# Routing of the last two fetched tiles moved from the decide stage into the dense stage

## What is computed

```
q  = (t @ wq) as 8 heads x 2 halves
sc = q . subkeys                      # 8 x 2 x 128 scores
sv, si = top_k(sc, 16)                # best 16 of each half
cand = sv[half 0][:, None] + sv[half 1][None, :]
cv, ci = top_k(cand, 16)
e  = si0[ci // 16] * 128 + si1[ci % 16]   # 8 x 16 expert numbers below 16384
g  = softmax(cv)
h  = u[e] . t ;  a = gelu(h) * g ;  out = sum a * v[e]
```

## Time and profile before

| | us |
|---|---|
| median of 3 runs | 4033.78 (4032.9 to 4043.76) |
| profiled execution | 4026.89 |
| its span | 4025.2 |

### The profile page before, as it was taken

One profiled execution on the slowest core, in us unless ns is written; L12 is line 12 of the kernel. 1 busy time (PEld: TensorE's weight loads), 2 busy tenths in 40 slices (PEclk: granted clock), 3 DMA queues, 4 the chain that ended last, 5 costly groups with the idle time before them and its releaser, 6 DMA issues. The chain is left out here.

```text
span 4025.2 us, 44686 instructions
## 1 busy us (share of the span) xinstructions
PE 3549.7 (88%) x14147; PEld 2107.2 (52%) x14147; DVE 2617.7 (65%) x5036; ACT 841.0 (21%) x1599; POOL 1631.8 (41%) x1245
## 2 busy tenths in 40 slices
PE   8997878776699999988862899999999999999998
PEld 6445567776457667656651344444444444444443
DVE  0451878883405435344464988888888878888886
ACT  1451211112423444354510000010001000010001
POOL 0000077770000777777773433334333334333331
PEclk9899889887799999999986999999999999999999
DMA  7793399995765656666856999999999999999994
GB/s 256 315 408 146 105 383 407 384 391 210 254 222 185 151 128 160 143 138 116 169 123 250 391 406 388 388 400 405 400 416 403 397 372 400 388 398 388 382 387 186
DMA packets 424246, 1201.21 MB, mean 298 GB/s; under 512 B 150473, under 2 KB 215417, under 8 KB 345337
## 3 DMA queue, kind: packets, MB, share of 16 engines
q0 software_dynamic: 168496, 680.80, 45.8%
q1 hardware_dynamic: 187600, 505.84, 34.2%
q10 hardware_dynamic: 67968, 12.45, 1.9%
HBM read 1127.33 MB, written 72.68 MB: 298 GB/s over the span
## 5 line engine op out<-in xcount | busy, mean ns | idle before, releaser
L2066 POOL DMA_INDIRECT d_ring<-peer_uv,d_idx x512 | 655.4, 1280 | 1087.6 <-DVEq L2120 981.9
L2223 PE MATMUL d_ps<-d_xd,d_u 128*128 128x512 f32 x2048 | 908.5, 597 | 99.9 <-DMA d_u<-u_blocks 81.1
L2234 PE MATMUL d_ps<-d_v,d_a 128*128 128x512 f32 x2048 | 914.1, 600 | 43.3 <-DVE d_a L2126 36.5
L1512 POOL DMA_INDIRECT G<-c_cellg,c_cell x384 | 617.5, 1608 | 436.6 <-DVE c_cellg L1641 233.5
L2118 DVE SCALAR_TENSOR_TENSOR d_acc<-d_ring,d_aw,d_acc 128x1024 f32<-128x1024 f32 x512 | 657.7, 1285 | 102.1 <-DVE d_acc L2118 66.9
L2223 PEld LDWEIGHTS d_ps<-d_xd,d_u 128*128 128x128 f32 x2048 | 391.8, 192 | 596.0 <-issue 584.3
L2234 PEld LDWEIGHTS d_ps<-d_v,d_a 128*128 128x128 f32 x2048 | 393.3, 193 | 545.5 <-issue 544.8
L2106 DVE SCALAR_TENSOR_TENSOR d_ring<-d_ring,d_xn 128x1024 f32<-128x1024 f32 x512 | 605.9, 1221 | 97.3 <-DMA d_qacc<-ys 51.5
L840 POOL DMA_INDIRECT a_x<-peer_uv,a_rowu x128 | 154.2, 1205 | 547.8 <-DVE a_rowv L910 505.3
L2188 ACT ACTIVATE d_ge<-d_h (+1 forms) x256 | 52.0, 203 | 1204.9 <-DVE d_ring L2106 1204.6
L1037 PE MATMUL a_ps<-a_w_low,a_x_high 128*128 128x256 f32 (+1 forms) x704 | 204.3, 290 | 61.7 <-DVE a_w_low L852 45.8
(11 more groups left out here) (360 smaller groups left out, 4134.4 us busy)
## 6 DMA issues: line engine op xcount, KB each, us to landing
c_chunk<-wq SPq DMA_DIRECT2D x128, 512.0 KB, 5.0
d_u<-u_blocks SPq DMA_DIRECT2D x128, 512.0 KB, 18.7
d_v<-v_blocks SPq DMA_DIRECT2D x128, 512.0 KB, 16.5
s_kc<-sb_kT SPq DMA_DIRECT2D x32, 1024.0 KB, 9.5
s_vc<-sb_v SPq DMA_DIRECT2D x32, 1024.0 KB, 7.4
c_chunk<-w_m SPq DMA_DIRECT2D x64, 512.0 KB, 5.5
d_gb<-G SPq DMA_DIRECT2D x32, 1024.0 KB, 34.5
G<-b_zeros SPq DMA_DIRECT2D x32, 768.0 KB, 8.3
```

The source lines that it names most:

```text
L1512: pool.indirect_dma_start(out=grid, out_offset=bass.IndirectOffsetOnAxis(ap=cell[q][:, s:s + 1], axis=0), in_=cell_g[q][:, s:s + 1], in_of ...
L2066: pool.indirect_dma_start(out=ring[:, b], out_offset=None, in_=a["peer_uv"], in_offset=bass.IndirectOffsetOnAxis(ap=idx8[par][:, b:b + 1], ...
L2223: last = nc.tensor.matmul(ps[:, HB + x % 2, :], ub[j][:, k], xd[:, k].rearrange("p t q -> p (t q)"), start=(k == 0), stop=(k == KC - 1))
L2234: last = nc.tensor.matmul(ps[:, VB + c % 4, :], A[u][j][:, q * P:(q + 1) * P], vb[u][j][:, half * 512:half * 512 + 512], start=(j == 0), s ...
```

## The change

VectorE no longer routes turns 7 and 8 in decide. ScalarE moves their scores into two tiles of their own (`late`), without waiting for VectorE, and stores them to memory, 1 MB each. In dense, ScalarE loads the first at the start and the second in block 14 into a tile that shares memory with the second token and sum buffers. VectorE runs the same routing steps in 15 pieces for each tile (`choose`), one at the end of each of blocks 0 to 14 (first of the two tiles) and 16 to 30 (second), writing into `idx` and `gw` directly. For that the first fetched tile is no longer a loop: its 32 blocks are written out on VectorE and ScalarE. The second tile's token and sum loads (`xn[1]`, `acc[1]`) wait until both tiles are routed (`chosen`). The results of gelu and weight are kept in place (`h`, `gw`) in place of tiles of their own. The third and fourth fetched tiles (GIVEN = 2 onwards) are the two concerned. SP's load of `gw` is cut to the first two tiles like that of `idx`, and the small table `digit` is loaded as well.

The 15 pieces of one tile are: 0 and 3, 16 max each; 1 and 4, 16 max_index; 2, 16 match_replace; 5, the three candidate sums; 6, 8 max and 8 max_index; 7, 8 match_replace and 8 max; 8, 8 max_index and the shift for the softmax; 9, ten small steps; 10 and 12, a one-hot test and its multiply over 2048 elements; 11 and 13, the reduction (13 also forms the expert number); 14, the sum, reciprocal and weights.

```diff
@@ decide @@
+        late = [sb(f"c_late{n}", [P, 16, P]) for n in range(2)]
 (SP)
-                routed(NT - 2)
-                routed(NT - 1)
 (VectorE)
                 normed(NT - 1)
-                halves_best(NT - 2)
-                pairs_best(NT - 2)
-                experts_of(NT - 2)
-                weigh(NT - 2)
-                halves_best(NT - 1)
-                pairs_best(NT - 1)
-                experts_of(NT - 1)
-                weigh(NT - 1)
 (ScalarE)
                 def scores_of(j):
-                    if j > 1:
+                    to = late[j - NT + 2] if j >= NT - 2 else sc
+                    if 1 < j < NT - 2:
                         act.wait_ge(dve_r.sem, dve_r.at(j - 1, "sum2"))
...
+                    if j >= NT - 2:
+                        act.wait_ge(act_r.sem, act_r.at(j, "sc3"))
+                        act.dma_start(o["late"][j - NT + 2], to[:]).then_inc(late_st, 16)
...
-                softmax(NT - 2)
                 scores_of(NT - 1)
-                softmax(NT - 1)
+                act.wait_ge(late_st, 32)
@@ dense @@
+        xa = sb("d_xa", [P, 4, D])
+        xn, acc = [xa[:, 0], xa[:, 2]], [xa[:, 1], xa[:, 3]]
+        late = xa[:, 2:4].rearrange("p u (r n) -> p (u r) n", n=P)
                 if T == 0:
-                    body(T, 0)
-                with eng.Fori(1 if T == 0 else 0, TB // BODY) as i:
-                    body(T, first + i)
+                    for k in range(TB // BODY):
+                        body(T, k)
+                else:
+                    with eng.Fori(0, TB // BODY) as i:
+                        body(T, first + i)
 (SP)
-                sp.dma_start(idx[:], o["idx"].rearrange("t p s -> p t s")).then_inc(rows_in, 16)
+                sp.dma_start(idx[:, 0:GIVEN], o["idx"][0:GIVEN].rearrange("t p s -> p t s")).then_inc(rows_in, 16)
 (GpSimd)
                 for T in range(FETCHED):
+                    if T >= GIVEN:
+                        pool.wait_ge(chosen, 2 * (T - GIVEN) + 1)
...
+                    if T == 0:
+                        pool.wait_ge(chosen, 4)
+                        pool.dma_start(xn[1], o["xn"][1]).then_inc(xn_in, 16)
+                        pool.dma_start(acc[1], o["ys"][DENSE + 1]).then_inc(acc_in, 16)
 (VectorE)
+                def choose(j, n):
...
+                    if n < 5:
+                        if n == 0:
+                            dve.wait_ge(eps_done, 3)
+                            dve.wait_ge(late_in, 16 * (j + 1))
+                        best(16, sc, top, top_i, ("top1", "cut", "top2", "topi"), j, n)
...
                             if m:
                                 add_rows(T, hb - 1, slots(m - 1), col - 2)
+                        if number(k):
+                            n = BODY * k + x
+                            choose(n // 16, n % 16)
 (ScalarE)
+                act.dma_start(late, o["late"][0]).then_inc(late_in, 16)
...
                         small_gelu(hb + 1, col + 2)
+                        if number(k) and BODY * k + x == 14:
+                            act.wait_ge(dve_r.sem, dve_r.at(0, "sum2"))
+                            act.dma_start(late, o["late"][1]).then_inc(late_in, 16)
+                        if number(k) and (BODY * k + x) % 16 == 9:
+                            j = (BODY * k + x) // 16
+                            act.wait_ge(dve_r.sem, dve_r.at(j, "shift"))
+                            nc.scalar.activation(gw[:, GIVEN + j], gw[:, GIVEN + j], ACT.Exp).then_inc(act_g, 1)
```

More of the change, by code:

```diff
@@ L1995, in dense @@
         prod_done, row_gelu, weighed, summed = sem("d_prod_done"), sem("d_row_gelu"), sem("d_weighed"), sem("d_summed")
+        chosen, late_in = sem("d_chosen"), sem("d_late_in")
+        dve_r = Steps(sem("d_dve_route"), "top1 cut top2 topi cand0 cand1 cand2 ctop1 ccut ctop2 ctopi shift "
+                      "topf mid high col low mid2 high2 rest place rise hot1 pick1 sum1 hot2 pick2 sum2 cell expert", 0)
+        act_g, dve_g = sem("d_act_softmax"), Steps(sem("d_dve_softmax"), "gsum grecip", 0)
         rms, recip, scaled = sem("d_rms"), sem("d_recip"), sem("d_scaled")
@@ L2042, in _ @@
                     v_rows(j, 0, j)
-                for dst, src in ((gw[:], o["gw"].rearrange("t p s -> p t s")), (gf[:], bass.AP(a["gf"].tensor, 0, [[0, P], [1, D]]))):
+                for dst, src in ((gw[:, 0:GIVEN], o["gw"][0:GIVEN].rearrange("t p s -> p t s")), (digit[:], a["digit"]), (gf[:], bass.AP(a["gf"].tensor, 0, [[0, P], [1, D]]))):
                     sp.dma_start(dst, src).then_inc(tabs, 16)
@@ L2099, in _, with step, best @@
                 dve.sem_inc(v_taken, LEAD)
-                dve.wait_ge(tabs, 32)
+                nc.vector.memset(top_f[:], 0.0).then_inc(eps_done, 1)
+                dve.wait_ge(tabs, 48)
+                def step(ins, j, name=None):
+                    ins.then_inc(dve_r.sem, 1)
+                    if name:
+                        dve.wait_ge(dve_r.sem, dve_r.at(j, name))
+                def best(n, src, vals, idx, names, j, stage):
+                    if stage == 0:
+                        for h in range(n):
+                            last = nc.vector.max(vals[:, h, 0:8], src[:, h])
+                        step(last, j, names[0])
+                    elif stage == 1:
+                        for h in range(n):
+                            nc.vector.max_index(idx[:, h, 0:8], vals[:, h, 0:8], src[:, h])
+                    elif stage == 2:
+                        for h in range(n):
+                            last = nc.vector.match_replace(src[:, h], vals[:, h, 0:8], src[:, h], LOW)
+                        step(last, j, names[1])
+                    elif stage == 3:
+                        for h in range(n):
+                            last = nc.vector.max(vals[:, h, 8:16], src[:, h])
+                        step(last, j, names[2])
+                    else:
+                        for h in range(n):
+                            last = nc.vector.max_index(idx[:, h, 8:16], vals[:, h, 8:16], src[:, h])
+                        step(last, j, names[3])
@@ L2140, in body @@
                         b = BODY * k + x
-                        if not (number(k) and x == 0):
+                        if not (number(k) and k == 0 and x == 0):
                             y = (x - 1) % BODY
```

97 lines of the change are left out of this document (78 added, 19 removed).

## The result

The changed kernel takes 4087.41 us in the median (4079.69 to 4090.63) against 4038.77 for the kernel before (4032.9 to 4044.38, measured beside it). The ratio is 1.0121, with a 95% interval of 1.0102 to 1.0141: **49 us slower**, between 41 and 57. Forecast were 4081 us and 47.5 us on top.

A forecast was written before the change was run, and what follows sets the result against it. TensorE was taken to set the dense stage's pace, with VectorE close behind and DMA nearly full. Starting VectorE 12.7 us earlier and adding 60.2 in the first tile gave +47.5 us, 4081 us in the median, range 4053 to 4115.

The forecast's parts named there:

- The first tile is VectorE's: First fetched tile: VectorE becomes the bound, 401.3 us of its own plus 93.0 + 3 for pieces; tile grows 60.2 us.
- The exit: End of decide: with the routing gone the scatters are late next; it comes about 14.7 us earlier, between 8 and 15.
- one of its own signs: End of decide, in the changed kernel's profile: wrong if the exit is later than 2142 or earlier than 2125.
- the 6.9 us of excess: End of decide: time of scatters and gaps over 1.54 and 0.3 us during VectorE's routing, forecast to go away.
- The opening: Start of dense: 2.6 us more for the score load, 0.6 less for index and weight tables, net +2.0 us.
- No cost in the other steps: First tile's Exp calls, second score load, delayed second-tile loads: 0 us; tiles two to four: no change, give or take 10.
- The relief: First fetched tile: straight code cuts VectorE's own time from 437.1 to 401.3 us, 35.8 us less.
- The scatters' excess staying (1): End of decide: long scatters stay long, so the exit gives 8 us in place of 14.7; 4088 us, chance 0.10.
- The pieces sinking into idle time (2): First fetched tile: VectorE's 62.2 us of idle time takes pieces, tile grows only 31 us; 4052 us, chance 0.06.
- The other side (3): First fetched tile: TensorE stays the bound because pieces cost under 48.5 us in place of 93; 4011 to 4021, chance 0.04.
- The clock (4): First fetched tile: TensorE's waits let its clock fall, 55 us on top; 4136 us, chance 0.05.
- Instruction supply (5): First fetched tile: long unrolled code pays a 6.6 us turn's worth some six times, 40 us; 4121 us, chance 0.05.

## Why the prediction was right, point by point

**The first tile is VectorE's: right.** 60.2 us of growth were forecast and 492.0 - 437.1 = 54.9 measured, and 492.0 to 492.3 in every profile that has the 30 pieces. The structure of the sum (401.3 us of its own, plus the pieces, against TensorE's bound) was tested from three sides: no pieces gives 427, half of them 446, all of them 492. The mis-sized term is the pieces: 93.0 + 3 us forecast, 492.0 - 401.3 = 90.7 measured, 45.4 a tile. Half of them gives nearly the same: 445.8 - 401.3 = 44.5. Most of the miss is the 3 us for the pieces' last waits, for which no time shows; the rest is the 46.5 us elapsed in the earlier trace rows, of which VectorE was busy for 45.6.

**The exit: right in kind, too large in size.** That the scatters are late next is shown by the pair with fewer of them. Forecast were 14.7 us (8 and 6.9 add up to 14.9). Measured are exits of 93.9, 86.2, 99.5, 87.0 and 88.4 us in the five profiles without routing there, against 102.4 to 103.4 in five with it: 3 to 17 us less, 12 in the mean (91.0 against 103.0). By one of its own signs the prediction failed: the first load was to go out between 2125 and 2142, and it went out at 2148.0 and 2151.3. The residual sum before it was 10 and 21 us later than in the trace that the forecast started from; but the sign made no room for that, nor did the forecast say how far the scatters follow it.

Three things were mis-sized.
- Behind the last scatter's start lie 6.4 us before the first load (2141.65 to 2148.03), where I had allowed 3. I had taken the gap of 2.01 us before the scatter at 2088.74 for a landing. But the program waits for landings only before the first of each 16 scatters, and this one is the ninth of its 16, the 361st in all. The gap stands there in all 12 profiles, with or without routing, and takes 1.9 to 5.9 us.
- For the same reason the 1.7 us of that gap, counted in the 6.9 us of excess, did not go away. The other 5.1, the long scatters themselves, did: after 2050 the first profile of the changed kernel has none over 1.54 us.
- I took a race between two chains to have one result. With the routing, the exit hangs on the residual sum and is always 102 to 103; without it, it hangs on scatters that began 730 us earlier, and moves with both.

**The opening: right.** 2.0 us were forecast. 51.3 to 51.7 us were measured in the profiles without the score load and 52.8 to 53.8 in those with it, 1 to 2.5 us more.

**No cost in the other steps: right for the first tile, off by 6 us behind it.** The kernel without pieces keeps all of them and has a tile of 427.1, against 427.9 with none of them. Behind the tile I forecast no change, give or take 10; it was 6 us more (1394.4 against 1388.4 in the means of two). The code there is the same, but its loops stand elsewhere in the program, and tile three shows instruction waits that it did not have.

**The sum** from two profiles of each: exit and opening -12, tile +56, rest +6, together +50; measured 49. It leaves out the last residual sum, which came 12 us later in the mean of the changed kernel's two profiles and which I take for chance. The medians bear that out: the kernel without pieces is 13 us under the one with the first tile written out, and with 3 us of it in the tile and behind it, 10 are left for exit less opening. The forecast of 47.5 came from -12.7 and +60.2. That it came within 2 us is luck: an error of 4 us on the tile and one of 6 on the rest cancelled. The forecast's own lower end, 4060, adds up to 4065 by its terms; nothing hangs on it.

**The relief** of 35.8 us fits as VectorE's own time and would have been wrong as a gain: 9 us of it show with the routing left in decide, since TensorE takes over at 428. With the pieces all of it counts.

**The rivals.** The scatters' excess staying (1) is out but for the 1.7 us of the gap. The pieces sinking into idle time (2), a tile 31 us longer, is out by the 54.9. The other side (3), TensorE as the bound, needed pieces below 48.5 us; they took 90.7. The clock (4): over the tile the mean granted clock fell from 0.97 to 0.93, so it was at the upper of its two levels (2.4 GHz) for most of the tile. TensorE's busy time there is 421.6 us against 414.7, and these 7 us lie within the time in which it waits for VectorE. Instruction supply (5): no idle time of that kind is in the written-out tile, and none in 128 blocks written out. It was the other way round: the loops waited for instructions.

## What to carry to other kernels

Moving work out of a stage's tail is worth the distance to what ends the stage next, here some 12 us of 59, and costs what it takes from the engine's slack at its new place: with bounds of 428 (TensorE) and 401 us (VectorE) in the tile, 91 us of pieces had room for 27. Work out both engines' own times before the move, and price moved instructions by their busy time. And where an engine has little slack, look first at the time between loop passes: writing the loops out gained 36 us, three times what the whole move gained at the exit.

## What the runs showed of the hardware

- A hardware loop's turn cost VectorE 5.8 to 7.1 us in some tiles and nothing in others, by the loop's place in the program. Tiles with that wait had 18 to 20 reads of instructions, the one without had 4. A block of the same work took 13.12 us in a loop and 12.61 written out.
- 128 written-out blocks ran without such a wait on VectorE while the DMA share was 0.96 at 388 GB/s.
- Scatters issued by GpSimd went from 1.54 to as much as 2.02 us beside VectorE multiplies of two tensors in SBUF and to 1.88 beside float32 copies, and stayed at 1.54 beside reductions and max.
- In all 12 profiles GpSimd stood idle for 1.9 to 5.9 us before the 361st scatter, whatever VectorE did; what it waits for was not found.
